# Attention in a diffusion backbone: six instead of four of ten key tiles of the probabilities turned by DMA

## The reference, cut to what matters

```python
def attention(q, k, v):
    ...
    def block(qi):
        s = jnp.einsum('bqhd,bkhd->bhqk', qi, k).astype(jnp.float32) * ATTN_SCALE
        pr = jax.nn.softmax(s, axis=-1).astype(v.dtype)
        return jnp.einsum('bhqk,bkhd->bqhd', pr, v)
```

## Time and profile before

| | us |
|---|---|
| time, median of 3 runs | 1535.19 (1534.98 to 1535.55) |
| the profiled execution | 1535.77 |
| its span | 1533.9 |
| PE busy | 1499.8 (98%) |
| DVE busy | 614.5 (40%) |
| ACT busy | 439.1 (29%) |
| POOL busy | 173.8 (11%) |

### The profile page before, as it was taken

One profiled execution on the slowest core, in us unless ns is written; L12 is line 12 of the kernel. 1 busy time (PEld: TensorE's weight loads), 2 busy tenths in 40 slices (PEclk: granted clock), 3 DMA queues, 4 the chain that ended last, 5 costly groups with the idle time before them and its releaser, 6 DMA issues.

```text
span 1533.9 us, 25610 instructions
## 1 busy us (share of the span) xinstructions
PE 1499.8 (98%) x10329; PEld 1196.6 (78%) x10329; DVE 614.5 (40%) x1393; ACT 439.1 (29%) x961; POOL 173.8 (11%) x172
## 2 busy tenths in 40 slices
PE   6999999999999999999999999999999999999997
PEld 3654545666666665544699999999999999999996
DVE  2211546675757685126784222222222222222215
ACT  2400102575757474334521111111111111111114
POOL 0005400121212122111000100100000000000000
PEclk9999999999999999999999999999999999999999
DMA  9970001233333262452586999999989999899875
GB/s 368 346 270 35 31 0 40 45 67 62 62 62 66 63 171 64 144 185 83 192 291 254 309 323 294 354 308 301 301 308 315 346 299 292 318 292 366 282 265 222
DMA packets 246331, 321.99 MB, mean 210 GB/s; under 512 B 141507, under 2 KB 143082, under 8 KB 244094
## 3 DMA queue, kind: packets, MB, share of 16 engines
q1 hardware_dynamic: 241230, 302.80, 59.4%
q0 software_dynamic: 4752, 17.30, 4.4%
q10 hardware_dynamic: 288, 1.05, 0.2%
HBM read 266.18 MB, written 21.64 MB: 188 GB/s over the span
## 4 chain that ended last, share of the span: by engine, by line
PE 89%; DVE 3%; DMA 3%; issue 3%; ACT 1%; POOL 1%; SPq 0%; DVEq 0%; ACTq 0%; POOLq 0%
PE ps L1277 32%; PE ps L1306 16%; PE ps L668 8%; PE ps L1007 8%; PE ps L905 6%; PE ps L956 4%; PE ps L693 2%; PE ps L939 2%; DMA wreg<-wreg 2%; PE ps L683 1%; PE ps L859 1%; PE ps L871 1%; PE ps L884 1%; PE ps L700 1%; DVE stat L1903 1%
## 5 line engine op out<-in xcount | busy, mean ns | idle before, releaser
L1277 PE MATMUL ps<-mreg,wreg 128*128 128x144 f32 x4096 | 506.3, 286 | 0.0
L1277 PEld LDWEIGHTS ps<-mreg,wreg 128*128 128x128 f32 x4096 | 503.4, 190 | 0.7 <-ACT hreg L1607 0.4
L1306 PE MATMUL ps<-mreg,wreg 128*128 128x144 f32 x2048 | 257.9, 287 | 2.3 <-DVE mreg L2344 2.3
L1306 PEld LDWEIGHTS ps<-mreg,wreg 128*128 128x128 f32 x2048 | 254.7, 191 | 2.5 <-DVE mreg L2344 2.5
L2344 DVE TENSOR_TENSOR mreg<-ps,mreg 128x144 f32<-128x144 f32 x128 | 39.4, 308 | 357.5 <-PE ps L1277 346.7
L905 PE MATMUL ps<-wreg 128*128 128x512 f32 (+2 forms) x400 | 168.3, 520 | 2.0 <-ACT hreg L1486 2.0
L1644 ACT ACTIVATE mreg<-ps 128x144 f32<-128x144 f32 x128 | 37.2, 291 | 426.1 <-PE ps L1277 426.1
L1007 PE MATMUL ps<-wreg,mreg 128*128 128x512 f32 x288 | 130.5, 598 | 0.0
L668 PE MATMUL ps<-hreg,wreg 128*128 128x512 f32 (+1 forms) x400 | 128.9, 480 | 0.0
L1903 DVE TENSOR_REDUCE stat<-ps 128x1 f32<-128x1280 f32 (+1 forms) x72 | 97.6, 1356 | 42.6 <-PE ps L905 42.5
L668 PEld LDWEIGHTS ps<-hreg,wreg 128*128 128x128 f32 x400 | 64.6, 191 | 62.2 <-issue 61.9
(11 more groups left out here) (307 smaller groups left out, 1272.3 us busy)
## 6 DMA issues: line engine op xcount, KB each, us to landing
wreg<-in_w_e_dram SPq DMA_DIRECT2D x96, 2048.0 KB, 12.0
wreg<-in_w_ada_dram SPq DMA_DIRECT2D x16, 1024.0 KB, 8.1
wreg<-in_w_ada_dram SPq DMA_DIRECT2D x16, 512.0 KB, 10.8
wreg<-in_w_out_dram SPq DMA_DIRECT2D x8, 512.0 KB, 4.1
wreg<-in_x_sample_dram SPq DMA_DIRECT2D x8, 512.0 KB, 4.3
x_rows<-wreg SPq DMA_DIRECT2D x8, 512.0 KB, 2.9
xn_rows<-wreg SPq DMA_DIRECT2D x8, 512.0 KB, 2.8
wreg<-x_rows SPq DMA_DIRECT2D x8, 512.0 KB, 8.8
```

Source lines behind the costliest of these rows:

```text
L1277: mm = pe.matmul(o[:, 0:CAP], w[s][:, k, (f % 4) * P:(f % 4 + 1) * P], xsT[b][:, k, :], start=(k == 0), stop=(k == KD - 1))
L1306: mm = pe.matmul(bank[4 + dm % 2][:, 0:CAP], w2[f // 4][:, f % 4, dm * P:(dm + 1) * P], hidT[:, f, :], start=(f == 0), stop=(f == 7))
```

## The change

The first six key tiles instead of four go by DMA (`TURNED` = 768 floats a row), and TensorE turns the remaining four into one bank, so that `ch` = 2 is gone. A split is cut into three copies of 256 floats each. The buffers of turned halves grow, and there are two instead of four, one for each head; SP therefore waits before a turn until the halves of n - 2 are joined (`turn_out(sp, i, n - 2, 0)`). One buffer of split halves lies in another place, over `new_out`, so GpSimd waits once until that has been stored. `weigh` takes tiles 6 to 9 first. The order on VectorE, and which engine joins which head, are as before.

```diff
-        prob_halves = [view(wreg, 23232 + s * 512, 512).bitcast(U16) for s in range(2)]
-        prob_halves_T = [view(wreg, 16384 + s * 512, 512)... for s in range(4)]
+        prob_halves = [view(wreg, at, TURNED).bitcast(U16) for at in (6784, 23232)]
+        prob_halves_T = [view(wreg, 16384 + s * D, TURNED)... for s in range(2)]
@@ join_prob
-            return copy(probT[:, 2 * (t % 2) + j, 0:512].bitcast(U16).rearrange("p (c h) -> p h c", h=2),
-                        prob_halves_T[n % 4].rearrange("p (h k) q -> p h (k q)", h=2))
+            return copy(probT[:, 2 * (t % 2) + j, 0:TURNED].bitcast(U16).rearrange("p (c h) -> p h c", h=2),
+                        prob_halves_T[n % 2].rearrange("p (h k) q -> p h (k q)", h=2))
@@ SP
             def turn_prob(i, n):
                 sp.wait_ge(halves_split, prob_split(i, n))
-                sp.dma_start_transpose(out=prob_halves_T[n % 4], in_=prob_halves[n % 2]).then_inc(...)
+                if n >= 2:
+                    turn_out(sp, i, n - 2, 0)
+                sp.dma_start_transpose(out=prob_halves_T[n % 2], in_=prob_halves[n % 2]).then_inc(...)
...
             for t in range(2):
-                turn_out(sp, 3, 12 + 2 * t, 0)
-                turn_out(sp, 3, 13 + 2 * t, 0)
+                turn_out(sp, 3, 14 + t, 0)
                 sp.dma_start(x_again[t], ...)
@@ TensorE
                 def turn(n, ch):
-                    if ch < 2:
-                        pe.wait_ge(norm_ok, i * 18 + n + 1)
+                    pe.wait_ge(norm_ok, i * 18 + n + 1)
                     bank_free(("turn", n, ch))
-                    for a in range(CHUNK_TILES[ch] if n < 16 else 1):
-                        kt = 4 * ch + a
+                    for a in range(4 if n < 16 else 1):
+                        kt = 6 * ch + a
...
-                    for kt in (4, 5, 6, 7, 8, 9, 0, 1, 2, 3) if t < NT - 1 else (10,):
-                        if kt == 8:
-                            turn_out(pe, i, 2 * t + 1, 2)
+                    for kt in (6, 7, 8, 9, 0, 1, 2, 3, 4, 5) if t < NT - 1 else (10,):
...
                     score(i, n, 1)
-                    turn(n - 2, 2)
                     score(i, n, 2)
...
@@ ScalarE
-                    turned(n - 2, 2)
                     exponential(n)
                     turned(n - 1, 1)
-                    turned(n - 1, 2)
@@ GpSimd
-                pool.tensor_copy(prob_halves[n % 2].rearrange("p (h k) -> p h k", h=2),
-                                 prob[n % 2][:, 0:512].bitcast(U16).rearrange("p (k h) -> p h k", h=2)).then_inc(halves_split, 1)
+                for k in range(0, TURNED, 256):
+                    ins = pool.tensor_copy(prob_halves[n % 2].rearrange("p (h k) -> p h k", h=2)[:, :, k:k + 256],
+                                           prob[n % 2][:, k:k + 256].bitcast(U16).rearrange("p (k h) -> p h k", h=2))
+                ins.then_inc(halves_split, 1)
+            pool.wait_ge(new_st, 32)
...
-CHUNK_TILES = (4, 4, 2)
+TURNED = 6 * P
-MID_ORDER = [u for n in range(2, 16, 2)
-             for u in [("turn", n - 2, 1), ("turn", n - 2, 2)] + [("weigh", (n - 4) // 2)][:n // 4]
-             + [("turn", n - 1, 1), ("turn", n - 1, 2)]]
+MID_ORDER = [u for n in range(2, 16, 2)
+             for u in [("turn", n - 2, 1)] + [("weigh", (n - 4) // 2)][:n // 4] + [("turn", n - 1, 1)]]
```

More of the change, by code:

```diff
@@ L202, in build @@
         rank_rows = view(wreg, 22528, QUICK, NS)
-        prob_halves = [view(wreg, 23232 + s * 512, 512).bitcast(U16) for s in range(2)]
-        prob_halves_T = [view(wreg, 16384 + s * 512, 512).bitcast(U16).rearrange("p (c q) -> p c q", q=P) for s in range(4)]
+        prob_halves = [view(wreg, at, TURNED).bitcast(U16) for at in (6784, 23232)]
+        prob_halves_T = [view(wreg, 16384 + s * D, TURNED).bitcast(U16).rearrange("p (c q) -> p c q", q=P) for s in range(2)]
         w1 = [view(wreg, s * 8192, KD, 512) for s in range(2)]
@@ L558, in turn_prob @@
                 sp.wait_ge(halves_split, prob_split(i, n))
-                sp.dma_start_transpose(out=prob_halves_T[n % 4], in_=prob_halves[n % 2]).then_inc((x_turned, y_turned)[n % 2], 16)
+                if n >= 2:
+                    turn_out(sp, i, n - 2, 0)
+                sp.dma_start_transpose(out=prob_halves_T[n % 2], in_=prob_halves[n % 2]).then_inc((x_turned, y_turned)[n % 2], 16)
             for i in range(3):
@@ L957, in weigh @@
                                            probT[:, 2 * (t % 2) + j, src * P:(src + 1) * P],
-                                           start=(kt in (4, 10)), stop=(kt in (3, 10)))
+                                           start=(kt in (6, 10)), stop=(kt in (5, 10)))
                     mm.then_inc(pv_mm, 1)
@@ L971, in attend @@
                     score(i, n + 1, 1)
-                    turn(n - 1, 2)
                     score(i, n + 1, 2)
@@ L977, in attend @@
                 turn(14, 1)
-                turn(14, 2)
                 score(i, 17, 0)
@@ L981, in attend @@
                 turn(15, 1)
-                turn(15, 2)
                 fill(2)
@@ L1465, in turned @@
                     t, j = divmod(n, 2)
-                    act.wait_ge(t_mm, i * 34 + turns_before(n, ch) + 1)
-                    w = CHUNK_TILES[ch] * P if n < 16 else P
-                    act.activation(probT[:, 2 * (t % 2) + j, ch * 512:ch * 512 + w], bank[MID_BANK[("turn", n, ch)]][:, 0:w],
+                    act.wait_ge(t_mm, i * 18 + n + 1)
+                    w = 512 if n < 16 else P
+                    act.activation(probT[:, 2 * (t % 2) + j, ch * TURNED:ch * TURNED + w], bank[MID_BANK[("turn", n, ch)]][:, 0:w],
                                    ACT.Copy).then_inc(t_out, 1)
@@ L1480, in exponential @@
                         if n < 16:
-                            act.wait_ge(t_mm, i * 34 + 2 * (n - 1))
+                            act.wait_ge(t_mm, i * 18 + n - 1)
                         act.wait_ge(halves_split, prob_split(i, n - 2))
@@ L1505, in attend @@
                 turned(14, 1)
-                turned(14, 2)
                 exponential(17)
                 turned(15, 1)
-                turned(15, 2)
                 turned(16, 0)
@@ L2584 @@
 V_BANK, V_TILES = (7, 6, 7), (4, 4, 3)
-CHUNK_TILES = (4, 4, 2)
 def o_bank(x):
     return (1, 2, 4, 5)[x] if x < 4 else 1 + x % 2
-def turns_before(n, ch):
-    return 2 * n + ch - 1 if n < 16 else 16 + n
 PROB_TURNS = 4 * 16
+TURNED = 6 * P
 DVE_JOINS = [(n, 0) for n in range(1, 16, 2)]
-ACT_TURNS = [u for n in range(2, 16, 2) for u in [(n - 4, 0)][:n // 4] + [(n - 2, 1), (n - 2, 2), (n - 1, 1), (n - 1, 2)]]
-ACT_TURNS += [(12, 0), (14, 0), (14, 1), (14, 2), (15, 1), (15, 2), (16, 0), (17, 0)]
+ACT_TURNS = [u for n in range(2, 16, 2) for u in [(n - 4, 0)][:n // 4] + [(n - 2, 1), (n - 1, 1)]]
+ACT_TURNS += [(12, 0), (14, 0), (14, 1), (15, 1), (16, 0), (17, 0)]
 MID_ORDER = [u for n in range(2, 16, 2)
-             for u in [("turn", n - 2, 1), ("turn", n - 2, 2)] + [("weigh", (n - 4) // 2)][:n // 4]
-             + [("turn", n - 1, 1), ("turn", n - 1, 2)]]
-MID_ORDER += [("weigh", 6)] + [("turn", n, ch) for n in (14, 15) for ch in (1, 2)]
+             for u in [("turn", n - 2, 1)] + [("weigh", (n - 4) // 2)][:n // 4] + [("turn", n - 1, 1)]]
+MID_ORDER += [("weigh", 6), ("turn", 14, 1), ("turn", 15, 1)]
 MID_ORDER += [("turn", 16, 0), ("turn", 17, 0), ("weigh", 7), ("weigh", 8)]
```

## The result

The changed kernel takes 1582.06 us (median of 4 runs, 1581.49 to 1586.75), the kernel before 1535.37 on the same chip (4 runs): ratio 1.0311 [1.029, 1.0331]. Predicted were 1580 and the range 1552 to 1598. The profiled execution took 1581.49, its span 1579.7.

What follows compares the result with a forecast made beforehand. The prediction took TensorE as the bound, with the odd heads' loop 0.45 us short of it; the longer loop would bind at 9.9 us. Three pairs at 11.95 plus 8.5 made +44.4 us, so 1580, range 1552 to 1598.

Steps and rivals of the forecast that it cites:

- The loop becomes the bound, at 9.9: Odd heads' round of split, DMA turn, join, maximum and scaling grows from 7.71 to 9.9 us; TensorE needs 7.71.
- Split 2.35: GpSimd's three copies for an odd head: 1.83 us plus 0.5 for VectorE's scaling coming in between; bounds 1.55 and 2.7.
- The first rival: The loop binds but GpSimd's parts run undisturbed: split 1.83, loop 9.4, +32 us, 1568; chance 0.25.
- Turn 3.7: DMA turn of 1536 half-words lands in 3.7 us instead of 3.1; bounds 3.4 and 4.3.
- Join 1.03: VectorE's join of 1536 half-words takes 1.03 us, 0.28 more than for 1024.
- One sign: TensorE idle in each 9.9 us round in the weighing's middle until the join, and before L939 until the scaling L1926.
- TensorE's 7.71 a round, 14 us in all: Dropped transposes cut TensorE's period from 8.15 to 7.71 us, 14 us off TensorE; the loop makes the saving idle.
- The new wait at nothing: SP's wait before a turn for the join of n-2 is over before need, so it costs nothing.
- First link +0.3: From scaling of head 1 to that of head 3 in each pair, only the longer join counts: +0.3 us.
- The end, 17.3 from scaling 13 to the turn of 16 and 17: End of the first three pairs: 17.3 us instead of 14.46 until TensorE turns tiles 16 and 17, +2.8 each.
- The last pair without that end: Last pair's end adds nothing, as output projections fill TensorE, and dropped transposes save 0.65: 8.5 us in all.
- The sum: Over four head pairs: three times 11.95 us plus 8.5 for the last, 44.4 us more.

Runs made afterwards that it cites:

- e11_new_order: Changed kernel with another written order on VectorE, TensorE and ScalarE, and tile 17 scaled ahead of the join of 15; 1531.96 us, ratio 0.9978 to the kernel before.
- the swap alone: Changed kernel with VectorE's scaling of tile 17 ahead of the join of 15 at a pair's end; 1575.44 us, ratio 1.026 to the kernel before.
- e12_new_order_copy: As e11_new_order, with each split in one GpSimd copy instead of three; 1531.55 us, ratio 0.9967 to the kernel before.

## Why the prediction was right

It was right in sign, cause and size, in the size with some luck. Step by step:

- *The loop becomes the bound, at 9.9.* Measured 9.86 to 9.87, and the chain has the predicted steps in the predicted order. Two errors of about 0.15 met in it: the loop before was shorter than I had it (7.54, not 7.71), the turn is longer. (The links were reckoned with 9.92, where the sum gives 9.90; that is 0.1 a pair.) That the written order closes it, and not the amount of work, is shown by e11_new_order: the same work with the same three copies has odd scalings 7.5 to 8.3 apart in the middle of the second pair, and with one copy the weighings above are 7.66 apart. That order differs on three engines at once; VectorE's alone (join, scaling, maximum) already brought the round to 8.3 to 8.7.
- *Split 2.35.* Measured 2.32. The parts of it were less exact: three copies alone take 1.72, not 1.83 (the fixed part of a copy is 0.13, not 0.18, from 1.72 against 1.46), and the handover costs 0.60, not 0.5. The first rival (undisturbed parts, 1568) falls by the 3.98 us that six copies take where twice 1.72 would be 3.44; both halves of the reading are shown by the one-copy kernel, and in the kernel before by the four-copy one. The Trainium skill's "SBUF — State Buffer", section "SBUF: two separate sides", says that VectorE in its fast modes and GpSimd share a pair of ports that is locked for a whole instruction; the 0.67 to 0.68 that the scaling needs after the copy's end, whether the copy is 1.04 or 1.46 long, agrees.
- *Turn 3.7.* Measured 3.9 (3.87 in the chain); this is the term that was too small. The prediction added nothing for the neighbouring turn. In the changed kernel the even head's turn is issued 1.67 us behind the odd one's; where it comes 2.21 behind (one copy) or 2.85 (join behind the maximum), the odd turn takes 3.70. That the neighbour is what lengthens it isn't shown by itself. Five links of 0.17 are nearly 1 us a pair.
- *Join 1.03.* Measured 1.04, with 62.9 us of idle time for the DMA before the 32 joins, as foretold. One sign did not come: in the rounds TensorE stands for the join alone and not before L939; the 6.0 us that it stands there for scalings are the ends of three pairs.
- *TensorE's 7.71 a round, 14 us in all.* It shows only where the loop is out of the way: 7.66 in the new order, with 8.8 us of the 14 gained at the last weighings.
- *The new wait at nothing.* Shown, 1580.78 without it.
- *First link +0.3.* 381.11 to 390.57 is 9.46, +0.2 on the 9.25 of before. Not foreseen: in three of four pairs one link took about 10.4, the turn landing late (4.40 to 4.46 us after its issue).
- *The end, 17.3 from scaling 13 to the turn of 16 and 17.* Measured 17.2 (440.80 to 458.01); the swap alone gives back 6.6 us, of which three waits of 2.0 are 6; +2.8 a pair were charged.
- *The last pair without that end.* Join 15 there starts at 652.85, the turn of 16 and 17 at 666.22, and the last weighings wait 0.35 as in before. But the 0.65 of saved transposes did not show: from the scaling of 13 to the last weighings it is 36.15 us instead of 35.82. In it lies the fall of the clock at 629 (24 matmuls take 2.83 there, 1.53 at 618.83).
- *The sum.* From the starts of the scalings in both traces: the first links of the four pairs lost 0.9 us together (forecast 1.2), the five plain links of each pair 35.4 in all (forecast 35.4), and all that stands behind the scaling of 13 lost 2.3, 4.4, 2.8 and 0.3 in the four pairs, 9.9 (forecast 7.75). That is 46.2; the first scaling of all comes 0.7 earlier than in before, so 45.6 at the last weighings, where 44.4 was forecast. The five links agree so well by luck: plain rounds of 9.86 would have made 34.2, and the late links, which I had not foreseen, made up for the rest. At the ends the forecast missed the clock: behind one of them eight matmuls take 4.92 instead of the 3.17 of before, 1.75 more.
- *What would make it wrong: a clock that falls.* It did fall, for some 4 us at one pair's end (458) and once in a round of the fourth pair (629), against my reading that it wouldn't; it cost some 3 us and not the prediction.

## What to carry to other kernels

Before giving a side path more work, measure how short of the bound it is: here the loop had some 0.6 us to spare, and the change asked for 2.3. Engines that issue in written order close loops that no data dependence asks for, so the loop must be followed through every engine whose order stands between its steps; four of my forecasts for a new order missed, by 21, 7, 15 and 9 us, because one engine was left out of the loop: TensorE in the first, ScalarE in the others. And an instruction cut in parts lets another engine in at a seam: here VectorE's scaling came in between the copies, and one copy instead of three was worth 27 us.

## What the hardware showed that I had not expected

The granted clock went from 1.00 (the 2.4 GHz level) to 0.50 (the 1.2 GHz level) for some 4 us behind single TensorE waits: in the changed kernel at 458 after 2.01 us and at 629 after 2.44, in e12_new_order_copy at 552 after 1.86. (The stretches shown have 0.54 to 0.64, since each takes in a piece at 1.00.) Yet the waits of 1.7 us every 9.9 us left it at 1.00, and so did six other waits of 1.96 to 2.44 in the same attention, among them those at the same end of two other pairs (2.02 at 363.61, 2.00 at 554.63). So the length of the wait alone doesn't tell whether the clock falls; what does wasn't tried. Where it fell at 458, the same eight matmuls took 1.55 times as long (4.92 for 3.17), so there a wait of 2 us cost near 4. And the kernels of the new order, quicker in the attention, scatter more (1526.96 to 1536.26) than the one before (1534.98 to 1537.54); of the eleven runs of e11_new_order those above 1533 us have a mean granted clock of 0.995 to 0.996, those below 1532 one of 0.996 to 0.997. The profile shown above had 2.4 us of its lead lost where the clock was low.
